# Two-block transformer kernel: the first modulation weights loaded into free rooms of the arena, and four chunks of the first projection multiplied between them

## The chip, the cores and the metric

The kernel runs on one core of a Trainium2 chip. The time is that of the device in microseconds, the median of a few executions. TensorE (PE in the profile) has two clock levels, 1.2 and 2.4 GHz.

## The reference

Two blocks follow one another on a sequence of 256 tokens of width 1024, all in float32. The first block has two layers. Each layer works on the 256 tokens `x` and on 256 context tokens `xc`, and each begins like this:

```python
shift, scale, gate = jnp.split(jax.nn.silu(c) @ p["w_ada"] + p["b_ada"], 3, axis=-1)
shift_c, scale_c, gate_c = jnp.split(jax.nn.silu(c_ctx) @ p["w_ada"] + p["b_ada"], 3, axis=-1)
h = _rmsnorm(x, p["norm_g"]) * (1.0 + scale[:, None, :]) + shift[:, None, :]
hc = _rmsnorm(xc, p["norm_g"]) * (1.0 + scale_c) + shift_c
hp = h @ p["w_in"]
```

`w_ada` is 1024 x 3072, `w_in` is 1024 x 2720. Then come a convolution branch, a Fourier branch, a gating branch and attention, an output projection and the gated residual. The second block has two layers of a gated feed-forward network, a mixer with sixteen heads, and another feed-forward network. The change touches only the first 50 us: from the first loads to the first two products with `w_in` of layer 0.

## The kernel before

**Tiles.** Features lie on the 128 partitions: `hT` holds the modulated input as 8 chunks (`KD` = 8) of 128 features by 512 tokens (256 of `x`, 256 of the context). A product of float32 precision is made of three products of split operands: each operand is a high part (rounded, `hH` for the input, `first_high` for weights) and a low part (`hL`, `first_low`, which lies in the place of the raw weights in the ring). `three` (L1893) issues high by high, high by low and low by high into one bank. ACT makes the high parts (`split_high`, L687, and L761, L763 for the input), DVE the low parts as the difference (`split_low`, L1196, and L1264). A plain float32 product of 128x512 is issued as one instruction and appears in the profile as two records.

**Loads.** All large weights go through `weight_ring`, three slots of 1 MB. SyncE (SP) fills them in the order of the list `SLOTS`; slot `n` waits until slot `n - 3` is used up (`fill`, L508). Layer 0 begins with eight slots of `w_ada` (the pairs `ADA_START` = 0, 4, 2, 6, two halves each), then come the slots of `w_in`, 256 columns each: first `a`, then `g`, `q`, `kv`/`kr` and so on. The small weights and constants are loaded by GpSimd (POOL), after it has seen `a` loaded (L586). `x` and the context are loaded by ScalarE's queue.

**Modulation.** For each pair of slots, PE multiplies silu(c) with it (`ada_half`, four products of 32 columns, L1877), ACT copies the result to SBUF (`ada_copy`, L685), PE transposes it (`ada_transposes`, L1890), DVE sums it (`ada_summed`, L1175). After two pairs one half of shift and scale is ready (`modulation`, L1192 and L1194): half 0, of pairs 0 and 4, serves the input chunks 0 to 3, half 1, of pairs 2 and 6, the chunks 4 to 7. Then ACT makes the even chunks of `hT` (L757, L758), DVE the odd ones (L1254, L1255), out of the transposes of the normalised rows, which PE makes (`x_transposes`, L1917) into the banks `XB`.

**PE's order** in layer 0 is written out by hand and each engine works strictly in its order:

```python
ada_products(*ADA_START[0]); ada_half(*ADA_START[1], 0); x_transposes([0, 1])
ada_half(*ADA_START[1], 1); ada_transposes(*ADA_START[0]); x_transposes([2, 3])
ada_transposes(*ADA_START[1]); ada_half(*ADA_START[2], 0); x_transposes([4])
ada_half(*ADA_START[2], 1); ada_half(*ADA_START[3], 0); ada_transposes(*ADA_START[2])
x_transposes([5]); ada_half(*ADA_START[3], 1); x_transposes([7])
ada_transposes(*ADA_START[3]); x_transposes([6]); warm(2)
```

(`;` stands for a line break here.) `warm(2)` is two plain products of the identity whose result nobody reads. After it `first_two` multiplies the two units of slot `a` (each 128 output features, 8 chunks of 3 products, 48 products in all), then the unit `g` follows, and so on.

Of the kernel before, what the change touches and what calls it, by code (L numbers as in the profile page):

```python
# [78 lines left out]
class Marks:  # L79


    def __init__(self, nc, ctx, table):
        self.nc, self.ctx, self.table = nc, ctx, table
        self.sems, self.counts = {}, {}
# [12 lines left out]
    def at(self, stage, *key):  # L97

        return self.sem(stage), self.table.get((stage,) + key, 1)
# [107 lines left out]
def program(nc, I, out, table):  # L207
    ctx = ExitStack()
    with ctx:
# [146 lines left out]

        def ada_slot(L, s):
            pair, q = s - s % 2, s % 2
            add(("ada", L, s), [(I["w_ada"][L][512 * q:512 * q + 512, 256 * pair:256 * pair + 512].rearrange("(k p) n -> p k n", p=P), ADA_WIDTH)])
# [8 lines left out]
        for L in range(2):  # L368
            win = [colslot(I["w_in"][L], c, n) for c, n in WIN_SLOTS]
            if L == 0:  # L370
                ada_slots(ADA_START)
# [48 lines left out]
        for L in range(2):  # L420
            for s in range(ADA_SLOTS):
                LAST[base[("ada", L, s)]] = ("ada_rows", L, s)
# [3 lines left out]
            for s in range(4):  # L426
                LAST[base[("wout", L)] + s] = ("wout_used", L, s, 1) if s < 3 else ("y_ready", "b1", L, 3 if L == 0 else 1, 1)
        def slot(n):
            return ring[:, n % RING, :]
# [77 lines left out]
        def _(sp):  # L507
# [61 lines left out]
            sp.wait_ge(M.sem("stored"), 64)  # L569
# [5 lines left out]
        def _(pool):  # L575
# [10 lines left out]
            pool.wait_ge(*filled(WIN[0, 0]))  # L586
# [84 lines left out]
        def _(act):  # L671
# [66 lines left out]
            def layer(L):  # L738
                nq = TT if L == 0 else T
                if L == 0:  # L740
                    norm(("b1", 0), range(4))
                    ada_copy(*ADA_START[0])
                    ada_copy(*ADA_START[1])
                else:
# [4 lines left out]
                for c in range(0, KD, 2) if L == 0 else ():  # L749
                    if c == 4:  # L750
                        ada_copy(*ADA_START[2])
                        ada_copy(*ADA_START[3])
                        split_high(0)
                        split_high(1)
# [4 lines left out]
                    if L == 0:  # L759
# [3 lines left out]
                        A(hH[:, c + 1, :], hT[:, c + 1, :], ACT.Copy).then_inc(*done("first_high", "input", c + 1))  # L763
                if L == 0:
# [393 lines left out]
        def _(dve):  # L1158
# [74 lines left out]
            def layer(L):  # L1233
# [616 lines left out]
        def _(pe):  # L1850
# [16 lines left out]
            def ada_half(L, s, q):  # L1867
# [6 lines left out]
                n = base[("ada", L, s + q)]  # L1874
                pe.wait_ge(*filled(n))
                for k in range(4):
                    last = mm(b[32 * k:32 * k + 32, :], CS[:, 4 * q + k, :], quarters(n)[:, k, :], start=(q == 0), stop=(q == 1), skip_group_check=True)  # L1877
# [29 lines left out]
            def layer(L):  # L1907
# [38 lines left out]

                if L == 0:
# [23 lines left out]
                hs = (hH, hL)  # L1971
# [11 lines left out]

                def first_two():
                    for j in range(2):
# [738 lines left out]
```

## Time and profile before

| | |
|---|---|
| median of 3 runs | 1441.98 us (1441.14 to 1442.56) |
| profiled execution: its own time | 1443.0 us |
| profiled execution: span of the core | 1441.2 us |
| PE busy | 1408.2 us, 98% of the span |
| VectorE (DVE) busy | 1004.8 us, 70% |
| ScalarE (ACT) busy | 717.2 us, 50% |
| GpSimd (POOL) busy | 72.1 us, 5% |
| granted clock of PE | 1.0 |

The span is the part of the execution that the profiler shows, 1.8 us shorter than the execution's own time. PE is busy nearly always. In the forty slices of the page only the first one (36 us) has it busy for half of the time.

### The profile page before, as it was taken

How to read it: one execution, taken by the hardware profiler on the slowest of the kernel's cores; microseconds unless marked ns; L12 is line 12 of the kernel's file. 1: busy time of each engine (PE TensorE's matmuls, PEld its weight loads, DVE VectorE, ACT ScalarE, POOL GpSimd, SP SyncE). 2: the span in 40 equal slices, each digit the busy share in tenths (PEclk: the TensorE clock that was granted, in tenths of full speed). 3: DMA queues.
4: the chain of work that ended last, by engine and by line, in shares of the span. 5: the costliest groups of instructions: out<-in, count | busy, mean ns of one | idle time of the engine just before them, and what ended most of it. 6: DMA issues, size and time to landing. Idle time of an engine off the chain costs nothing.

```text
span 1441.2 us, 22052 instructions
## 1 busy us (share of the span) xinstructions
PE 1408.2 (98%) x8031; PEld 1158.1 (80%) x8031; DVE 1004.8 (70%) x1669; ACT 717.2 (50%) x1228; POOL 72.1 (5%) x98
## 2 busy tenths in 40 slices
PE   5999999999999999999999999999999999999998
PEld 2768747869748888888878888888888888888887
DVE  2588455459547777787687777777777876877776
ACT  4433155345445444485764444654444756644444
POOL 0300211200110000000100000000000002000000
PEclk9999999999999999999999999999999999999999
DMA  9623175364235766554445556646665643455662
GB/s 344 210 88 88 59 254 192 99 198 143 88 118 165 245 194 202 196 184 125 146 132 175 175 178 201 203 145 198 201 199 175 191 140 124 132 175 176 202 201 91
DMA packets 185653, 243.28 MB, mean 169 GB/s; under 512 B 4560, under 2 KB 154608, under 8 KB 185456
## 3 DMA queue, kind: packets, MB, share of 16 engines
q1 hardware_dynamic: 182272, 229.43, 49.2%
q0 software_dynamic: 2736, 10.82, 2.2%
q10 hardware_dynamic: 576, 2.10, 0.4%
q8 instruction: 45, 0.74, 0.2%
q14 instruction: 24, 0.20, 0.0%
HBM read 241.27 MB, written 1.05 MB: 168 GB/s over the span
## 4 chain that ended last, share of the span: by engine, by line
PE 86%; DMA 4%; DVE 4%; ACT 3%; issue 2%; SPq 0%; POOL 0%; DVEq 0%; ACTq 0%; POOLq 0%
PE bank L1896 41%; PE bank L2412 18%; PE bank L2414 9%; DMA weight_ring<-in_w_ffn_up 2%; PE bank L2023 2%; PE bank L2304 2%; ACT weights_high L941 2%; DVE weights_low L1492 1%; DMA weight_ring<-in_w_ada 1%; PE bank L1877 1%; PE bank L2245 1%; PE bank L2168 1%; PE bank L2270 1%; PE bank L2254 1%; PE bank L2576 1%
## 5 line engine op out<-in xcount | busy, mean ns | idle before, releaser
L1492 DVE TENSOR_TENSOR weights_low<-weight_ring,weights_high 128x1024 fp32r<-128x1024 f32 x328 | 392.9, 1222 | 126.0 <-ACT weights_high L941 125.8
L941 ACT ACTIVATE weights_high<-weight_ring 128x1024 fp32r<-128x1024 f32 x328 | 334.6, 1048 | 100.4 <-PE bank L1896 62.0
L2412 PE MATMUL bank<-input_split,weights_high 128*128 128x512 f32 x1280 | 319.5, 391 | 0.0
L2412 PEld LDWEIGHTS bank<-input_split,weights_high 128*128 128x128 f32 x1280 | 234.7, 188 | 44.9
L2414 PEld LDWEIGHTS bank<-input_split,weights_low 128*128 128x128 f32 x1280 | 174.6, 190 | 12.5
L2414 PE MATMUL bank<-input_split,weights_low 128*128 128x256 f32 x1280 | 178.5, 282 | 0.0
L1896 PE MATMUL bank<-weights_high,hidden_high 128*128 128x512 f32 x352 | 138.7, 394 | 4.0 <-DVE hidden_low L1601 4.0
L1015 ACT ACTIVATE silu_gate<-gate_sum 128x256 f32<-128x256 f32 x88 | 36.8, 418 | 204.0 <-DVE gate_sum L1579 200.1
L1896 PE MATMUL bank<-weights_low,hidden_high 128*128 128x512 f32 x352 | 137.9, 392 | 0.0
L1896 PE MATMUL bank<-weights_high,hidden_low 128*128 128x512 f32 x352 | 137.0, 389 | 0.0
L1896 PE MATMUL bank<-input_split,weights_high 128*128 128x256 f32 x576 | 105.6, 285 | 0.0
L1021 ACT ACTIVATE hidden_high<-hidden 128x256 fp32r<-128x256 f32 x88 | 36.8, 418 | 131.4 <-DVE hidden L1592 124.4
L1896 PE MATMUL bank<-hT_high,first_high 128*128 128x512 f32 (+1 forms) x248 | 89.9, 362 | 1.3 <-DVE weight_ring_low L1198 1.1
L1896 PE MATMUL bank<-weights_high,input_split 128*128 128x256 f32 (+1 forms) x384 | 90.3, 323 | 0.5 <-issue 0.5
L1896 PEld LDWEIGHTS bank<-input_split,weights_high 128*128 128x128 f32 x576 | 89.5, 192 | 1.1 <-DVE qk_feature_major L1675 0.7
L1896 PE MATMUL bank<-hT_high,weight_ring_low 128*128 128x512 f32 (+1 forms) x248 | 86.9, 350 | 0.0
L1896 PE MATMUL bank<-input_split,weights_low 128*128 128x256 f32 x288 | 81.4, 283 | 0.0
L1896 PEld LDWEIGHTS bank<-weights_high,hidden_high 128*128 128x128 f32 x352 | 66.4, 189 | 17.1 <-issue 5.6
L1896 PEld LDWEIGHTS bank<-weights_high,hidden_low 128*128 128x128 f32 x352 | 66.1, 188 | 14.4
L1896 PEld LDWEIGHTS bank<-weights_low,hidden_high 128*128 128x128 f32 x352 | 66.4, 189 | 10.6
L1896 PEld LDWEIGHTS bank<-weights_high,input_split 128*128 128x128 f32 x384 | 64.4, 190 | 8.6 <-issue 3.5
L1601 DVE TENSOR_TENSOR hidden_low<-hidden,hidden_high 128x256 fp32r<-128x256 f32 x88 | 37.4, 425 | 43.7 <-ACT hidden_high L1021 43.7
(337 smaller groups left out, 2218.3 us busy)
## 6 DMA issues: line engine op xcount, KB each, us to landing
weight_ring<-in_w_ffn_gate SPq DMA_DIRECT2D x44, 1024.0 KB, 5.2
weight_ring<-in_w_ffn_up SPq DMA_DIRECT2D x44, 1024.0 KB, 5.3
weight_ring<-in_w_ffn_down SPq DMA_DIRECT2D x44, 1024.0 KB, 4.9
weight_ring<-in_w_in SPq DMA_DIRECT2D x32, 1024.0 KB, 5.3
weight_ring<-in_w_ada SPq DMA_DIRECT2D x24, 1024.0 KB, 5.7
weight_ring<-in_w_out SPq DMA_DIRECT2D x16, 1024.0 KB, 4.9
weight_ring<-in_w_in SPq DMA_DIRECT2D x24, 512.0 KB, 5.1
gain_row<-in_norm_gains POOLq DMA_DIRECT2D x6, 512.0 KB, 3.8
```

The costliest lines, as they stand in the source:

```text
L941: A(unit_in(WH, U), unit_source(U), ACT.Copy).then_inc(s_high, 1)
L1015: A(sgate[:, par, :], gsum[:, par, :], ACT.Silu).then_inc(s_silu, 1)
L1021: A(HBH[:, par if to is None else to, :], hbuf[:, par, :], ACT.Copy).then_inc(s_hh, 1)
L1492: TTn(unit_in(WL, U), unit_source(U), unit_in(WH, U).bitcast(F32), ALU.subtract).then_inc(s_low, 1)
L1601: TTn(HBL[:, to, :], hbuf[:, par, :], HBH[:, to, :].bitcast(F32), ALU.subtract).then_inc(s_hl, 1)
L1877: last = mm(b[32 * k:32 * k + 32, :], CS[:, 4 * q + k, :], quarters(n)[:, k, :], start=(q == 0), stop=(q == 1), skip_group_check=True)
L1896: last = mm(o, lhs(x), rhs(y), start=start and m == 0, stop=stop and m == 2, skip_group_check=True)
L2023: last = mm(b[out_rows, 0:ncol], lhs(k), hT[:, k, 0:ncol], start=(k == 0), stop=(k == KD - 1))
L2168: last = mm(b[:, sg * T:(sg + 1) * T], FA[:, 2 * sg + tl, m, cs * P:(cs + 1) * P], dft_n[:, cs, tl, :], start=(g == 0), stop=(g == 3))
L2304: last = mm(o, SG[:, k, tok], rows(n)[:, r, half], start=start, stop=final, skip_group_check=True)
L2412: mm(b[:, :].rearrange("p (h n) -> p h n", h=2), unit_in(WH, U)[:, k, :], HX[:, k, :, :], start=(k == 0), stop=False, skip_group_check=True)
L2414: last = mm(b[:, 0:T], unit_in(WL, U)[:, k, :], HH[:, k, :], start=False, stop=(k == KD - 1), skip_group_check=True)
```

## The change

The eight slots of `w_ada` for the start leave the ring. They go to five rooms of 2048 columns of `arena`, which hold nothing yet at this time: the first five need no wait, each of the last three waits until the slot five before it is multiplied. SP's order becomes: modulation slots 0 to 3, `a`, modulation slots 4 to 7, the constants `ones`, then `g` and `q` (no wait, as the ring is empty), then the others. POOL's loads now wait for the last modulation product and not for `a`. Five existing semaphores count the loads of the rooms; those who wait on them later add what the rooms have counted.

PE multiplies the first four input chunks with both units of `a` between the modulation products, in the order shown below. The transposes of chunk 7 move ahead of the last modulation half, `warm(2)` becomes five such products into bank 6, and after them the chunks 4 to 7 follow. ACT splits unit 0 of `a` before chunk 0 and unit 1 after the chunks 0 and 1, DVE makes the low parts in the same places, and `ada_summed` of the third pair moves to the fourth.

```diff
@@ loads
+        START = [(L, s + q) for L, s in ADA_START for q in range(2)]
+        START_ROOM = [arena[:, a:a + 2048] for a in (3840, 5888, 9592, 11640, 13688)]
+        START_SEMS = ("softplus_masked", "scores2", "p2_T", "pT2_ready", "stored")
...
+            def fill_start(i):
+                L, s = START[i]
+                if i >= 5:
+                    sp.wait_ge(*at("ada_rows", *START[i - 5]))
+                sp.dma_start(start_slot(i), ada_source(L, s)).then_inc(start_loaded[i % 5], 16)
+
+            for i in range(4):
+                fill_start(i)
             n_first = base[("ffn", 0)]
             for n in range(n_first):
                 fill(n, *SLOTS[n])
                 if n == WIN[0, 0]:
+                    for i in range(4, 8):
+                        fill_start(i)
                     sp.dma_start(KB[:, P:C_PICK], I["k_base"][:, P:C_PICK]).then_inc(M.sem("ones_loaded"), 16)
...
-            pool.wait_ge(*filled(WIN[0, 0]))
+            pool.wait_ge(*at("ada_rows", *START[-1]))
@@ ACT
                     ada_copy(*ADA_START[0])
                     ada_copy(*ADA_START[1])
+                    split_high(0)
...
                     if c == 4:
                         ada_copy(*ADA_START[2])
                         ada_copy(*ADA_START[3])
-                        split_high(0)
-                        split_high(1)
...
                         A(hH[:, c + 1, :], hT[:, c + 1, :], ACT.Copy).then_inc(*done("first_high", "input", c + 1))
+                        if c == 0:
+                            split_high(1)
@@ DVE
                     if L == 0 and c == 5:
+                        ada_summed(*ADA_START[2])
                         ada_summed(*ADA_START[3])
                         modulation(0, 1)
-                        split_low(0)
...
-                    if L == 0 and c == 3:
-                        ada_summed(*ADA_START[2])
-                    if L == 0 and c == 5:
-                        split_low(1)
+                    if L == 0 and c == 1:
+                        split_low(0)
...
+                    if L == 0 and c == 1:
+                        split_low(1)
@@ PE
+                def first_two(chunks, units=(0, 1)):
+                    w = [(first_high(j), first_low(j)) for j in range(2)]
+                    for j in units:
+                        if chunks[0] == 0:
+                            for r in hand_over(PB[0]["a", j], ("a_ready", 0, j)):
+                                pe.wait_ge(*at(*r))
+                            pe.wait_ge(*at("first_low", "weight", j))
+                        for k in chunks:
+                            pe.wait_ge(*at("first_low", "input", k))
+                            last = three(B[PB[0]["a", j]][:, :], lambda x: w[j][x][:, k, :], lambda y: hs[y][:, k, :], k == 0, k == KD - 1)
...
                     ada_transposes(*ADA_START[1])
+                    x_transposes([4])
                     ada_half(*ADA_START[2], 0)
-                    x_transposes([4])
+                    first_two((0, 1))
                     ada_half(*ADA_START[2], 1)
                     ada_half(*ADA_START[3], 0)
                     ada_transposes(*ADA_START[2])
                     x_transposes([5])
+                    x_transposes([7])
+                    first_two((2,))
                     ada_half(*ADA_START[3], 1)
-                    x_transposes([7])
+                    first_two((3,), (0,))
                     ada_transposes(*ADA_START[3])
+                    first_two((3,), (1,))
                     x_transposes([6])
-                    for r in hand_over(2):
+                    for r in hand_over(6):
                         pe.wait_ge(*at(*r))
-                    warm(2)
+                    for _ in range(5):
+                        mm(B[6][:, :], ident, X[:, 0, 0:512], start=True, stop=True)
+                    first_two((4, 5))
+                    first_two((6, 7))
```

## Rows read from the trace of the kernel before

**Rows 1.** The waits of PE over the whole span: us, times, longest us.

```profile
PE bank L1864 <- DMA const_base<-in_k_base: 9.7, 1, 9.7
PE bank L1877 <- DMA weight_ring<-in_w_ada: 4.3, 5, 1.8
PE bank L1896 <- DVE hidden_low L1601: 4.0, 3, 1.9
PE bank L1890 <- ACT ada_rows L685: 2.0, 2, 1.8
...
PE bank L1896 <- DVE weight_ring_low L1198: 1.1, 1, 1.1
```

**Rows 2.** The chain that ended last, in order of time: start, us.

```profile
4.51 13.13 DMA weight_ring<-in_w_ada
...
28.25 7.53 DMA weight_ring<-in_w_in
...
38.38 39.09 PE bank L1896 x168
```

**Rows 3.** Timeline of PE: start, us; idle before and its releaser in brackets.

```profile
21.55 1.94 PE L1877 MATMUL bank<-weight_ring,silu_c 128*32 128x512 f32 x8
...
26.54 0.66 PE L1917 MATMUL bank<-const_base,gated 128*128 128x128 f32 x4
27.13 1.07 PE L1877 MATMUL bank<-weight_ring,silu_c 128*32 128x512 f32 x8
28.78 1.07 PE L1877 MATMUL bank<-weight_ring,silu_c 128*32 128x512 f32 x8 [0.59 <-DMA weight_ring<-in_w_ada]
31.64 0.63 PE L1890 MATMUL bank<-const_base,ada_rows 128*128 128x128 f32 x4 [1.79 <-ACT ada_rows L685]
32.10 0.60 PE L1917 MATMUL bank<-const_base,gated 128*128 128x128 f32 x4
32.63 1.06 PE L1877 MATMUL bank<-weight_ring,silu_c 128*32 128x512 f32 x8
33.63 0.66 PE L1917 MATMUL bank<-const_base,gated 128*128 128x128 f32 x4
34.51 0.63 PE L1890 MATMUL bank<-const_base,ada_rows 128*128 128x128 f32 x4 [0.22 <-ACT ada_rows L685]
34.98 0.60 PE L1917 MATMUL bank<-const_base,gated 128*128 128x128 f32 x4
35.41 1.88 PE L1937 MATMUL bank<-residual,const_base 128*128 128x512 f32 x4
38.38 0.47 PE L1896 MATMUL bank<-hT_high,first_high 128*128 128x512 f32 x1 [1.08 <-DVE weight_ring_low L1198]
...
49.53 0.39 PE L1896 MATMUL bank<-hT_high,first_high 128*128 128x512 f32 x1
```

**Rows 4.** Stretches: us, busy PE, PEld, DVE, ACT, POOL, then granted clock, DMA share, GB/s.

```profile
20.00:24.00 4.00, 4.00 (x19) 2.00 (x18) 0.00 (x0) 0.45 (x1) 0.00 (x0) 1.00 1.05 388
24.00:28.00 4.00, 4.00 (x35) 2.11 (x33) 1.72 (x6) 1.68 (x4) 0.00 (x0) 1.00 1.03 342
28.00:32.00 4.00, 1.62 (x16) 0.58 (x13) 2.20 (x4) 3.28 (x7) 0.00 (x0) 1.00 0.98 307
```

**Rows 5.** Timelines of SP, then of ACT and DVE, 14 to 38 us.

```profile
14.36 0.37 SPq L518 DMA_DIRECT2D weight_ring<-in_w_ada  x1
...
23.55 0.60 ACT L685 ACTIVATE ada_rows<-bank 128x512 f32<-128x512 f32 x1 [4.87 <-PE bank L1877]
26.37 0.54 DVE L1254 TENSOR_SCALAR hT<-bank,ada_gain,ada 128x256 f32<-128x256 f32 x1
26.43 0.57 ACT L757 ACTIVATE hT<-bank,ada,ada_gain 128x256 f32<-128x256 f32 x1 [2.29 <-DVE ada_gain L1194]
27.48 0.63 ACT L761 ACTIVATE hT_high<-hT 128x512 fp32r<-128x512 f32 x1
28.14 1.29 DVE L1264 TENSOR_TENSOR hT_low<-hT,hT_high 128x512 fp32r<-128x512 f32 x2 [0.78 <-ACT hT_high L761]
35.68 0.17 DVE L1194 SCALAR_TENSOR_TENSOR ada_gain<-ada,vectors_T 128x8 f32<-128x8 f32 x1
35.81 2.00 ACT L691 ACTIVATE first_high<-weight_ring 128x1024 fp32r<-128x1024 f32 x2 [1.45 <-DMA weight_ring<-in_w_in]
36.90 1.23 DVE L1198 TENSOR_TENSOR weight_ring_low<-weight_ring,first_high 128x1024 fp32r<-128x1024 f32 x1 [1.05 <-ACT first_high L691]
```

**Rows 6.** Load issued at 14.36 us: KB, us from issue to landing.

```profile
weight_ring<-in_w_ada SPq DMA_DIRECT2D x1, 1024.0 KB, 6.0
```

More of the change, by code:

```diff
@@ L83, in __init__ @@
         self.nc, self.ctx, self.table = nc, ctx, table
-        self.sems, self.counts = {}, {}
+        self.sems, self.counts, self.start_count = {}, {}, {}
     def sem(self, stage):
@@ L355, in rows2, with ada_source @@
             return w.rearrange("(s r p) n -> s p r n", r=2, p=P)[s], 0
+        def ada_source(L, s):
+            pair, q = s - s % 2, s % 2
+            return I["w_ada"][L][512 * q:512 * q + 512, 256 * pair:256 * pair + 512].rearrange("(k p) n -> p k n", p=P)
         def ada_slot(L, s):
[L358 to L359 removed]
+            add(("ada", L, s), [(ada_source(L, s), ADA_WIDTH)])
         def ada_slots(pairs):
@@ L420, in program @@
         for L in range(2):
-            for s in range(ADA_SLOTS):
+            for s in range(8 if L == 0 else 0, ADA_SLOTS):
                 LAST[base[("ada", L, s)]] = ("ada_rows", L, s)
@@ L427, in program, with start_slot, start_filled @@
                 LAST[base[("wout", L)] + s] = ("wout_used", L, s, 1) if s < 3 else ("y_ready", "b1", L, 3 if L == 0 else 1, 1)
+        START = [(L, s + q) for L, s in ADA_START for q in range(2)]
+        START_ROOM = [arena[:, a:a + 2048] for a in (3840, 5888, 9592, 11640, 13688)]
+        START_SEMS = ("softplus_masked", "scores2", "p2_T", "pT2_ready", "stored")
+        start_loaded = [M.sem(stage) for stage in START_SEMS]
+        for i in range(len(START)):
+            M.start_count[START_SEMS[i % 5]] = 16 * (i // 5 + 1)
+        def start_slot(i):
+            return START_ROOM[i % 5].rearrange("p (k n) -> p k n", k=4)
+        def start_filled(i):
+            return start_loaded[i % 5], 16 * (i // 5 + 1)
         def slot(n):
@@ L1873, in ada_half @@
                 b = B[ADA_BANK[L, s]]
-                n = base[("ada", L, s + q)]
-                pe.wait_ge(*filled(n))
+                if (L, s) in ADA_START:
+                    i = START.index((L, s + q))
+                    pe.wait_ge(*start_filled(i))
+                    rows4 = start_slot(i)
+                else:
+                    pe.wait_ge(*filled(base[("ada", L, s + q)]))
+                    rows4 = quarters(base[("ada", L, s + q)])
                 for k in range(4):
-                    last = mm(b[32 * k:32 * k + 32, :], CS[:, 4 * q + k, :], quarters(n)[:, k, :], start=(q == 0), stop=(q == 1), skip_group_check=True)
+                    last = mm(b[32 * k:32 * k + 32, :], CS[:, 4 * q + k, :], rows4[:, k, :], start=(q == 0), stop=(q == 1), skip_group_check=True)
                 last.then_inc(*done("ada_rows", L, s + q))
@@ L1945, in spatial_transposes @@
                     last.then_inc(*done("ws_transposed", L))
+                hs = (hH, hL)
+                def first_two(chunks, units=(0, 1)):
[8 more added lines that the diff above has]
+                            last = three(B[PB[0]["a", j]][:, :], lambda x: w[j][x][:, k, :], lambda y: hs[y][:, k, :], k == 0, k == KD - 1)
+                        if chunks[-1] == KD - 1:
+                            last.then_inc(*done("proj", 0, "a", j))
                 if L == 0:
@@ L1982, in project_split @@
                     last.then_inc(*done("proj", 0, *key))
-                def first_two():
-                    for j in range(2):
-                        for r in hand_over(PB[0]["a", j], ("a_ready", 0, j)):
-                            pe.wait_ge(*at(*r))
-                    w = [(first_high(j), first_low(j)) for j in range(2)]
-                    for k, j in [(k, j) for ks in (range(0, 4), range(4, 6), range(6, 8)) for j in range(2) for k in ks]:
-                        if k == 0:
-                            pe.wait_ge(*at("first_low", "weight", j))
-                        if j == 0:
-                            pe.wait_ge(*at("first_low", "input", k))
-                        last = three(B[PB[0]["a", j]][:, :], lambda x: w[j][x][:, k, :], lambda y: hs[y][:, k, :], k == 0, k == KD - 1)
-                        if k == KD - 1:
-                            last.then_inc(*done("proj", 0, "a", j))
                 def project(name, j, n, lhs, out_rows, ncol, reader, first=False):
```

8 lines of the change are left out of this document (2 added, 6 removed).

## The prediction

> **What bounds the kernel now.** I read the waits of PE first [rows 1]. PE is busy 98% of the span, so only what shortens or lengthens PE's own order counts. Of its waits, 9.7 us are for the first constants and not touched. The change is aimed at some of the others, which lie in the first 40 us. The chain of waits [rows 2] shows why they are there. The chain runs through the loads, ends its last load with slot `a` landing at 28.25 + 7.53 = 35.78, passes through the split of unit 0, and from 38.38 on it is PE without a break for 39.09 us. Whatever moves PE's arrival at unit `g` (49.53, the last row of [rows 3]) moves the rest by the same amount. The later waits on the ring hang on PE's own releases, so they move along. I therefore build PE's new timeline up to unit `g` and compare it with 49.53.
>
> The stretches [rows 4] show that the loads run at 388 GB/s until 24 us and sag to 307 by 32: the ring of three makes SP wait for products. The timeline of PE [rows 3] shows what it does meanwhile. Its idle time after 25 us: 0.59 before the record at 28.78, 1.79 before 31.64, 0.22 before 34.51 and 1.1 before 38.38, some 3.7 us in all. That is the most the change can win here. Part of it is already used by two plain products: four records of 1.88 us together.
>
> **Where the loads land.** Row by row the third load lands at 4.51 + 13.13 = 17.64 [rows 2] and the fourth at 14.36 + 6.0 = 20.4 [rows 5, 6]: one megabyte per 2.72 us, which is 1.05 MB at 386 GB/s. The new order has no hole, so `a`, fifth in line, lands at 23.1, modulation slots 4 to 7 at 25.8, 28.5, 31.3 and 34.0, `ones` at 34.7, `g` at 37.5. The last modulation slot is thus later than in the old order (its product started at 32.63), since a megabyte was put ahead of it.
>
> **Up to the first early product.** Until 25.5 us nothing changes on PE. Then chunk 4's transposes (0.5) and modulation slot 4 (landed at 25.8, eight records, 1.07) end at about 27.1. The first early product needs the low parts of unit 0 and of chunk 0.
> ACT: the copy of the second pair ends at 23.55 + 0.60 = 24.15; the split of unit 0 takes 1.0 and ends at 25.25, before the gain is ready at 26.34, so it is hidden, with 1.1 us to spare if `a` should land later. hT of chunk 0 starts at 26.43, the high part at 27.48, that of chunk 1 ends at 28.63 [rows 5]. The split of unit 1 then ends at 29.7.
> DVE: chunk 1 from 26.37 to 27.36; low part of unit 0, 1.23, to 28.6; low parts of chunks 0 and 1, 0.65 each, to 29.25 and 29.9; low part of unit 1 needs ACT's at 29.7 and ends at 31.15.
> So PE starts unit 0 at 29.35, after 2.2 us idle, ends its two chunks at 30.75, waits 0.45 and starts unit 1 at 31.2. Behind that wait stand all later modulation products, although slot 5 lies ready since 28.5 us.
>
> **From 31.2 on PE has no hole.** Prices: 48 split products took 49.53 - 38.38 = 11.15 us, 0.232 each; a modulation half 1.04; transposes of a pair 0.45 and of a chunk 0.5 (starts of neighbouring rows); a plain product two records 0.43 apart, 0.86 [rows 3].
>
> - unit 1, chunks 0 and 1: 6 x 0.232 = 1.39, to 32.6
> - modulation slots 5 and 6: 2.08, to 34.7 (landed at 28.5 and 31.3; the copy of the third pair, from 33.7 to 34.35, is hidden by slot 6)
> - transposes of the third pair and of chunks 5 and 7: 1.45, to 36.15
> - chunk 2, both units: 1.39, to 37.55 (its low part is ready near 33 us, as ACT and DVE have nothing else)
> - modulation slot 7: 1.04, to 38.6. It landed at 34.0, so a delay of the loads up to 3.5 us costs nothing
> - chunk 3, unit 0: 0.70, to 39.3, which hides ACT's copy of 0.60
> - transposes of the last pair 0.45, chunk 3 of unit 1 0.70, transposes of chunk 6 0.45: to 40.9
> - five plain products: 5 x 0.86 = 4.3, to 45.2
> - chunks 4 to 7: 24 x 0.232 = 5.57, to 50.8
>
> That is 1.25 us later than 49.53.
>
> **Do the plain products fill a pause?** Chunk 4's low part is late by this chain: transposes of the last pair start at 39.3; in the old trace from there to the gain is 35.85 - 34.51 = 1.34 us; from the gain to chunk 4's low part is what it was for chunk 0: from 26.34 to 28.14 + 0.65 = 28.8, 2.45 us. ACT is free for it now, since the weight splits that took it from 35.81 to 37.81 are gone from this place. So chunk 4 is ready at 43.1. PE is free at 40.9. The pause is 2.2 us long and the products put into it last 4.3: they overfill it by 2.1 us. Without any of them PE would go on at 43.1 and reach `g` at 48.7, 0.8 us before the old time. Chunks 5 to 7 become ready in time: ACT and DVE need some 5.3 us from the gain to chunk 7, and PE asks for chunk 6 at 48.0.
>
> In terms of work: PE saves about 1.3 us of idle time, and gets three plain products more, 2.6 us.
>
> **Behind it.** The splits of unit `g` follow chunk 7 on ACT: near 45.3 to 47.4, low parts to 48.8, needed at 50.8: hidden. `g` and `q` land at about 37.5 and 40 to 42, before their splits. In the old order `q` landed near 49.6 and PE did not wait for it either, so the earlier landing wins nothing. POOL's small loads start after 38.6 and not at 36.08, 2.5 us later; nobody waited for them. SP's queue has no wait before slot `kv` that PE could feel. The rest keeps its order: shift +1.25 us.
>
> **The clock.** All stretches show a granted clock of 1.00 [rows 4], that is 2.4 GHz, but eight modulation records take 1.94 us at 21.55 and 1.07 at 27.13 [rows 3]; I go by the durations, which have the lower level before 24 us and the upper one after it. Between 27.13 and 31.64 the old order gave PE only sparse modulation products and 2.4 us of idle time, and the transposes at 31.64 still ran fast. The new hole from 27.1 to 29.35 is shorter than that stretch, so I take no fall. The Trainium skill ("TensorE: Matmul & The Clock Gate", the part on the clock gate) says that the throttled level is the default and that sustained activity releases it, which speaks for plain products in a pause and against a hole ahead of dense work; if it bit here the time would be that of the second rival below.
>
> **The rivals.**
>
> *First: the early chunks start earlier than I have them (gain).* If DVE and ACT fed PE from 27.1 on without a hole, the 12 products would end at 29.9, not 32.6, and slot 7 still lands in time (34.0 against 34.9), so `g` starts at 48.1: -1.4 us, 1440.6. For it: slot 4 is done at 27.1 and nothing else stands in PE's way. Against it: low parts cannot be there before 29.25 by the rows of ACT and DVE. Part of it, 0.5 us from a quicker unit 1, is thinkable.
>
> *Second: the clock falls in the hole at 27.1 (slower than before).* Place: the products from 29.35 on. Price: in the old trace the level rose after PE had been busy from 19.65 to 24, 4.3 us; that much work at half the rate adds 2.2 us, on top of 1.25: +3.4, 1445.4. It decides from 1.6 us of slow work's extra on. For it: 2.2 us idle after a sparse half. Against it: the old stretch named above, and the even longer sparse one after 28.
>
> *Third: the low parts come later than by my rows,* because ACT and DVE run into each other's waits or `a` lands late, after 24.2. Each microsecond beyond 1.1 of a late `a` shifts PE by one. At 2 us late, and a chunk 4 still covered by the plain products, 1444.2.
>
> *Fourth: something outside this window,* for example a ring or a queue that now runs half a step better or worse. No row speaks for it; both signs.
>
> **How the numbers follow.** The profiled execution took 1443.0, 1.0 above the median of 1441.98; its shift goes onto the median: 1441.98 + 1.25 = 1443.2 us. Chances: this case 0.62 (1442.4 to 1444.2); first rival, in whole or in part, 0.17 (1440.6 to 1442.4); second 0.08 (1444.6 to 1446.5); third 0.08 (1444 to 1446); fourth 0.05. A change of 0.2%, 2.9 us, is about what a measurement tells from none. My case lies within it. Slower by more than that needs the second rival or a strong third: 0.11. Faster by more is beyond the 1.4 us that PE's order can give and is left to the fourth and to an error in my timeline: 0.07. The range that holds 8 in 10 is 1440.9 to 1445.0.
>
> **What would show it right or wrong.** In the new profile: `a` landing near 23 and slot 7 near 34 us; the first early product at 29.3, unit 1's at 31.2; slot 7's product at 37.5, not at its landing; ten records of plain products from 40.9 to 45.2 with chunk 4's low part ready at 43.1, two us before they end; unit `g` at 50.8 without a wait. I am wrong if the low part of chunk 4 is later than the last plain product (then the pause was real and my chain from the last pair is too short), if eight modulation records take 1.9 us after 29, or if PE waits anew behind 50 us.

## The result, and the profile after

The changed kernel takes 1443.26 us (median of 22 runs, 1441.98 to 1446.42), the kernel before 1440.97 us (22 runs, 1439.47 to 1443.88). The ratio is 1.0016, with a 95% interval of 1.001 to 1.0022: 2.3 us slower (1.4 to 3.2 us by the interval). The forecast was 1443.2 us, a shift of 1.25 us. The time came out where it was forecast, but the shift is nearly twice as large and the forecast one lies just under the interval: the kernel before was 1.0 us faster over 22 runs than over the first three, and the forecast leaned on those three. One of the twelve executions of e1 below took 4949.69 us; it counts in e1's median and not in its ratio.

The timeline of PE in the profiled execution after (start, us; idle before in brackets), which answers to [rows 3]. L1907 is the modulation product, L1926 the split product, L1920 and L1947 the transposes, L2017 the five plain products:

```profile
21.55 1.44 PE L1907 MATMUL bank<-arena,silu_c 128*32 128x512 f32 x8
...
24.28 0.60 PE L1920 MATMUL bank<-const_base,ada_rows 128*128 128x128 f32 x4
...
26.23 1.07 PE L1907 MATMUL bank<-arena,silu_c 128*32 128x512 f32 x8 [0.91 <-DMA arena<-in_w_ada]
28.51 0.47 PE L1926 MATMUL bank<-hT_high,first_high 128*128 128x512 f32 x1 [1.22 <-DVE hT_low L1287]
...
31.74 1.92 PE L1907 MATMUL bank<-arena,silu_c 128*32 128x512 f32 x16
33.61 0.64 PE L1920 MATMUL bank<-const_base,ada_rows 128*128 128x128 f32 x4
34.09 1.04 PE L1947 MATMUL bank<-const_base,gated 128*128 128x128 f32 x8
...
36.45 1.06 PE L1907 MATMUL bank<-arena,silu_c 128*32 128x512 f32 x8
...
38.33 0.63 PE L1920 MATMUL bank<-const_base,ada_rows 128*128 128x128 f32 x4
...
39.50 0.60 PE L1947 MATMUL bank<-const_base,gated 128*128 128x128 f32 x4
39.93 4.46 PE L2017 MATMUL bank<-residual,const_base 128*128 128x512 f32 x10
43.83 0.79 PE L1926 MATMUL bank<-hT_high,first_high 128*128 128x512 f32 x1
...
49.78 0.39 PE L1926 MATMUL bank<-hT_high,first_high 128*128 128x512 f32 x1
```

PE waits 0.91 us for modulation slot 4, before 26.23, and 1.22 us before 28.51; from there on no wait is listed until unit `g` at 49.78 us. The forecast had one wait of 2.2 us behind slot 4; the slot came later than forecast (issued at 11.62 and 14.5 us on its way, so landed at 26.1, where 25.8 was forecast) and now splits it in two. The ten records of the five plain products run from 39.93 to past 44. The same execution's timeline of DVE shows when chunk 4 was ready:

```profile
41.48 1.29 DVE L1287 TENSOR_TENSOR hT_low<-hT,hT_high 128x512 fp32r<-128x512 f32 x2 [0.78 <-ACT hT_high L784]
```

Two low parts in 1.29 us: chunk 4's is there at 42.13, half of that later. PE was free for it at 39.93. The pause is 2.2 us long and is filled with 4.3 us.

The last modulation slot is issued at 20.54 us by the timeline of SP:

```profile
20.54 1.81 SPq L543 DMA_DIRECT2D arena<-in_w_ada  x1
```

and the view of the loads gives its time from issue to landing:

```profile
arena<-in_w_ada SPq DMA_DIRECT2D x1, 1024.0 KB, 13.7
```

It lands at 34.24 us and is multiplied at 36.45, because chunk 2's products stand in front of it.

Unit `g` starts only 0.25 us later than in [rows 3] (49.78 against 49.53). Part of that is luck of this execution. The eight modulation records at 21.55 took 1.44 us and not 1.94, and the transposes that start at 24.28 above stand at 25.02 in the timeline of PE before:

```profile
25.02 0.60 PE L1890 MATMUL bank<-const_base,ada_rows 128*128 128x128 f32 x4
```

So PE became fast earlier than in the profile of before, by about 1.5 us (an estimate: twice the 0.74 us by which it is ahead, as it works at half the rate until then). Single profiles are compared below only where the same row tells when the clock rose. Nor does the shift of 0.25 us simply run through to the end. In the chain of this pair it is 0.24 us at 96 us and 0.31 at 453; by 490 us, behind a stretch in which the chain runs through a load of `in_w_ffn_up`, it is -0.14, and at 1421 us -0.59.

A good marker of the end of the products with `a` is ACT's first read of their banks, 1.2 us ahead of unit `g`. In the timeline of ACT, before and after:

```profile
48.36 0.60 ACT L774 ACTIVATE arena<-bank 128x512 f32<-128x512 f32 x1 [3.53 <-PE bank L1896]
48.60 0.60 ACT L799 ACTIVATE arena<-bank 128x512 f32<-128x512 f32 x1 [2.35 <-PE bank L1926]
```

### The profile page after: what moved, and what is told of

Same layout as the page of the kernel before. It is cut to its first block, busy times and chain, and to the rows that moved or that the text cites. A ratio compares the mean times of both kernels' runs of the same rounds, so it can differ in the third digit from the quotient of the medians.

```text
span 1440.6 us, 22065 instructions
## 1 busy us (share of the span) xinstructions
PE 1409.9 (98%) x8037; PEld 1158.9 (80%) x8037; DVE 1005.4 (70%) x1669; ACT 717.3 (50%) x1228; POOL 72.1 (5%) x98
## 3 DMA queue, kind: packets, MB, share of 16 engines
HBM read 241.27 MB, written 1.05 MB: 168 GB/s over the span
## 4 chain that ended last, share of the span: by engine, by line
PE 86%; DVE 5%; ACT 3%; DMA 3%; issue 2%; SPq 0%; POOL 0%; DVEq 0%; ACTq 0%; POOLq 0%
PE bank L1926 41%; PE bank L2447 18%; PE bank L2449 9%; PE bank L2059 2%; DMA weight_ring<-in_w_ffn_up 2%; PE bank L2339 2%; DVE weights_low L1517 1%; ACT weights_high L966 1%; PE bank L1907 1%; PE bank L2280 1%; DMA arena<-in_w_ada 1%; PE bank L2203 1%; PE bank L2305 1%; PE bank L2289 1%; PE bank L2611 1%
## 5 line engine op out<-in xcount | busy, mean ns | idle before, releaser
L1926 PE MATMUL bank<-weights_high,hidden_high 128*128 128x512 f32 x352 | 138.7, 394 | 3.1 <-DVE hidden_low L1626 3.1
L1926 PE MATMUL bank<-weights_low,hidden_high 128*128 128x512 f32 x352 | 137.9, 392 | 0.0
L1926 PE MATMUL bank<-weights_high,hidden_low 128*128 128x512 f32 x352 | 137.0, 389 | 0.0
L1926 PE MATMUL bank<-input_split,weights_high 128*128 128x256 f32 x576 | 105.6, 285 | 0.0
L1926 PE MATMUL bank<-hT_high,first_high 128*128 128x512 f32 (+1 forms) x248 | 90.7, 366 | 1.4 <-DVE hT_low L1287 1.2
L1926 PE MATMUL bank<-weights_high,input_split 128*128 128x256 f32 (+1 forms) x384 | 90.2, 323 | 0.5 <-issue 0.5
L1926 PEld LDWEIGHTS bank<-input_split,weights_high 128*128 128x128 f32 x576 | 89.6, 192 | 1.1 <-DVE qk_feature_major L1700 0.7
L1926 PE MATMUL bank<-hT_high,weight_ring_low 128*128 128x512 f32 (+1 forms) x248 | 86.9, 350 | 0.0
L1926 PE MATMUL bank<-input_split,weights_low 128*128 128x256 f32 x288 | 81.4, 283 | 0.0
L1926 PEld LDWEIGHTS bank<-weights_high,hidden_high 128*128 128x128 f32 x352 | 66.4, 189 | 16.2 <-issue 4.6
L1926 PEld LDWEIGHTS bank<-weights_high,hidden_low 128*128 128x128 f32 x352 | 66.1, 188 | 14.4
L1926 PEld LDWEIGHTS bank<-weights_low,hidden_high 128*128 128x128 f32 x352 | 66.4, 189 | 10.6
L1926 PEld LDWEIGHTS bank<-weights_high,input_split 128*128 128x128 f32 x384 | 64.4, 190 | 8.6 <-issue 3.5
```

Source lines behind the costliest of these rows:

```text
L1926: last = mm(o, lhs(x), rhs(y), start=start and m == 0, stop=stop and m == 2, skip_group_check=True)
```

## The experiments

Eleven runs, nine altered kernels and both kernels once more, stand in three groups (e1 to e4, e5 to e8, e9 to e11), each group on one chip and in five rounds beside the kernel before. The marker is ACT's first read of unit `a`'s bank; "eight records" is the length of the modulation product at 21.6 us, 1.94 where the clock rose late. Each execution also has a mean granted clock, rounded to 0.001; an estimate of its worth is at most 1.4 us for each 0.001, as 0.001 of 1441 us of PE's time. At most, since it also holds the last 2 to 3 us, where PE runs out of work and the clock falls too (0.97 from 1420 to 1440 us in the first profile after, 1.00 in the one before).

| | median us | ratio (95% interval) | marker us | eight records us |
|---|---|---|---|---|
| before (first profile) | | | 48.36 | 1.94 |
| after (first profile) | 1443.26 | 1.0016 (1.001 to 1.0022) | 48.60 | 1.44 |
| e1 no plain product | 1442.59 | 1.0005 (0.9995 to 1.0014) | 49.02 | 1.94 |
| e2 two plain | 1441.25 | 1.0000 (0.999 to 1.001) | 47.35 | 1.94 |
| e3 before, five plain | 1443.98 | 1.0017 (1.0008 to 1.0027) | 49.07 | 1.63 |
| e4 slot 7 first | 1440.15 | 0.9994 (0.9986 to 1.0003) | 46.00 | 1.91 |
| e5 after, again | 1443.71 | 1.0015 (1.0006 to 1.0024) | 49.72 | 1.21 |
| e6 before, again | 1441.76 | 1.0003 (0.9994 to 1.0012) | 47.91 | 1.62 |
| e7 slots 5 and 7 first | 1440.59 | 0.9987 (0.9978 to 0.9996) | 47.23 | 1.26 |
| e8 products late | 1442.83 | 1.0006 (0.9997 to 1.0015) | 49.80 | 1.94 |
| e9 one in the hole | 1442.64 | 1.0002 (0.9992 to 1.0011) | 48.61 | 1.36 |
| e10 slot 7 first, held | 1440.17 | 0.9983 (0.9974 to 0.9991) | 45.52 | 1.56 |
| e11 late, held | 1442.19 | 0.9993 (0.9985 to 1.0002) | 47.31 | 1.33 |

The kernel before has a median of its own in each group (1441.69, 1441.90 and 1442.15), so the ratios are to be compared, not the medians.

### e1 and e2: how many plain products the pause wants

```diff
-                    for _ in range(5):
+                    for _ in range(0):   # e1; range(2) in e2
```

> The changed kernel without any of the five plain products in the pause. Theory A (the pause is 2.2 us and the five products of 0.86 us overfill it): in the profile of after PE reaches the pause at 39.93 us and chunk 4's low part is ready at 42.13, while the products end near 44.2; without them the next split product starts at 42.1 to 42.3 and everything behind moves by 2.1 us: about 1441.2 us, ratio to before 0.9995 to 1.0005. Rival B (the products keep the clock up): PE falls to the lower level in the empty 2.2 us, the 24 split products behind it take more than 0.25 us each at first, and the time is no better than with five, 1443 us or more. Rival C (the slowdown comes from elsewhere, later than 50 us): the unit g starts 2.1 us earlier in the profile, but the time stays at 1.0016 of before.

> The changed kernel with two plain products in the pause, as many as before the change. Theory A: two products last 1.72 us, from 39.93 to 41.65, less than the pause, so the time is that of the kernel without any, 2.1 us under the changed one: about 1441.2 us. If Rival B holds, two are better than none by the cost of the fallen clock, 1 us or more.

With two, the ratio is 1.0000: 1.6 thousandths under the changed kernel, 2.3 us, where 2.1 was expected. PE waits 0.41 us behind the two products, and the marker stands at 47.35, with the late rise, 1.0 us ahead of before; no gain over the kernel before shows in the time. With none, the pause is as long (a wait of 2.23 us, below), but the times fall into two heaps, seven from 1440.3 to 1442.9 and four from 1444.7 to 1445.3. The profile is of the upper heap (1445.13 us). Its stretches (us, busy PE, PEld, DVE, ACT, POOL, then granted clock, DMA share, GB/s) show the clock falling behind the pause:

```profile
43.00:44.00 1.00, 0.98 (x4) 0.85 (x5) 1.00 (x3) 0.97 (x3) 1.00 (x3) 1.00 0.97 391
44.00:45.00 1.00, 1.00 (x4) 0.77 (x3) 0.98 (x2) 0.83 (x3) 1.00 (x2) 0.58 0.94 287
45.00:46.00 1.00, 1.00 (x3) 0.74 (x3) 0.69 (x1) 1.00 (x3) 1.00 (x3) 0.50 0.72 129
46.00:47.00 1.00, 1.00 (x4) 0.77 (x3) 0.96 (x1) 0.94 (x2) 1.00 (x3) 0.50 1.09 223
47.00:48.00 1.00, 1.00 (x5) 0.83 (x4) 1.00 (x2) 0.00 (x0) 1.00 (x2) 0.71 0.81 195
```

and the timeline of PE in it shows the price:

```profile
43.02 0.47 PE L1926 MATMUL bank<-hT_high,first_high 128*128 128x512 f32 x1 [2.23 <-DVE hT_low L1287]
...
45.18 0.63 PE L1926 MATMUL bank<-hT_low,first_high 128*128 128x512 f32 x1
45.60 0.63 PE L1926 MATMUL bank<-hT_high,weight_ring_low 128*128 128x512 f32 x1
46.03 0.63 PE L1926 MATMUL bank<-hT_high,first_high 128*128 128x512 f32 x1
```

Split products are 0.43 us apart instead of 0.23, for some 3.3 us: the clock fell to 1.2 GHz after the empty pause. Marker 49.02 against 47.35 in e2, 1.7 us for it. The pause doesn't explain the heaps, though. The same profile has a second fall, behind a wait of PE in the later block:

```profile
506.88 0.49 PE L1926 MATMUL bank<-weights_high,hidden_high 128*128 128x512 f32 x1 [2.00 <-DVE hidden_low L1626]
```

```profile
508.00:510.00 2.00, 2.00 (x7) 1.57 (x6) 2.00 (x3) 0.19 (x1) 0.00 (x0) 0.59 0.94 313
510.00:512.00 2.00, 2.00 (x6) 1.53 (x5) 1.68 (x4) 0.55 (x2) 0.00 (x0) 0.55 0.93 304
```

And ten of the eleven executions have a mean clock of 0.998 or less, against 11 of the 35 of the kernel before, so the first fall probably belongs to most of them, those of the lower heap too. So Theory A holds for the length of the pause, and Rival B for the clock in it: plain products in the pause are worth having, two do it, three more are paid in full.

### e3: the plain products alone

```diff
-                    warm(2)
+                    warm(5)
```

> The kernel before with five plain products in place of two, nothing else of the change. Theory A: in the old trace two products end at 37.1 us and the first split product starts at 38.38; five would end at 35.41 + 4.3 = 39.7, so +1.3 us: 1442.3 us, ratio 1.0009. If plain products are worth something for the clock in this pause, the time is that of before or under it.

1.0017; the interval from 1.0008 holds the expected 1.0009 just. In the profile the marker is 49.07 against 47.91 in e6, whose clock rose at the same time: +1.16 us. Three more of them cost what they last, less the rest of the pause, in the old kernel too. The time moved by about twice that, 2.4 us by the ratio, with a granted clock of 1.00 in its profile from the rise to 1440 us. So a time that moves by more than the marker isn't peculiar to the changed kernel.

### e4: the order of PE

```diff
-                    first_two((2,))
                     ada_half(*ADA_START[3], 1)
-                    first_two((3,), (0,))
+                    first_two((2,), (0,))
                     ada_transposes(*ADA_START[3])
-                    first_two((3,), (1,))
+                    first_two((2,), (1,))
+                    first_two((3,))
...
-                    for _ in range(5):
+                    for _ in range(0):
```

> The changed kernel with no plain product and with the last modulation half ahead of chunk 2's products; the products of chunks 2 and 3 then stand behind it and cover the chain from its transposes to chunk 4. Theory A': PE is the bound from 28.5 us on and what was badly used was the order. Slot 7 landed at 34.2 us, its product starts at 34.9 and not at 36.45, its pair's transposes near 36.6, chunk 4's low part is ready near 40.4, PE is free at 39.4 to 39.7. So about 0.9 us of pause remain and unit g starts near 46.3 us, 3.3 us before the kernel before: about 1437.7 us, ratio 0.9977, 1.4 us or so under the version without plain products. Rival B: the clock falls in the holes and the time is above 1440. Rival C: the start of unit g moves but the time does not.

The timeline of PE in e4 shows the last modulation product earlier:

```profile
35.71 1.06 PE L1907 MATMUL bank<-arena,silu_c 128*32 128x512 f32 x8
...
37.58 0.63 PE L1920 MATMUL bank<-const_base,ada_rows 128*128 128x128 f32 x4
```

With the late rise the marker is 46.00, 2.4 us before the old one and 1.35 before e2 (expected 1.4). In the time the ratio is 0.9994: the expected 0.9977 lies outside the interval. The gain at the marker is real, but the time doesn't show it clear of noise; four of the twelve executions took 1441.9 to 1443.2.

### e5 and e6: both kernels once more

> The changed kernel once more, unaltered, beside the controls of this call. Theory D (the forecast's shift of 1.0 to 1.3 us is right and the measured 2.3 us is scatter of the later stages): ratio near 1.0009. Theory E (the clock also falls or rises late in some executions of it, as it did at 44 us without plain products): ratio again 1.0014 to 1.0020, with two heaps of times 2 us apart.

> The kernel before, unaltered: a control of how far two equal kernels come out apart. Expected ratio 1.0000, within 0.0005. Its profile is a second look at the old timeline: if the clock rises earlier than 24 us there, unit a ends earlier by as much of it as the loads do not absorb.

The control gives 1.0003. Its clock rose earlier than in the first profile of the same kernel, PE is 0.54 us ahead at 25 us, and the marker is 0.45 us earlier: the loads absorb little of it. The changed kernel gives 1.0015 again (the interval, from 1.0006, also holds the forecast 1.0009), so a slowdown of this order isn't scatter of one group. Its second profile shows what the first did not, in the same view of stretches:

```profile
27.00:28.00 1.00, 0.33 (x4) 0.00 (x0) 1.00 (x2) 1.00 (x3) 0.00 (x0) 1.00 1.06 389
28.00:29.00 1.00, 0.66 (x3) 0.54 (x4) 1.00 (x3) 1.00 (x2) 0.00 (x0) 0.89 1.06 391
29.00:30.00 1.00, 1.00 (x4) 0.81 (x3) 1.00 (x2) 0.97 (x3) 0.00 (x0) 0.50 1.05 385
30.00:31.00 1.00, 1.00 (x4) 0.80 (x3) 1.00 (x3) 0.36 (x2) 0.00 (x0) 0.50 1.05 387
31.00:32.00 1.00, 1.00 (x4) 0.72 (x3) 0.90 (x2) 0.51 (x1) 0.00 (x0) 0.50 1.05 389
```

and the timeline of PE in that profile:

```profile
28.34 0.47 PE L1926 MATMUL bank<-hT_high,first_high 128*128 128x512 f32 x1 [1.01 <-DVE hT_low L1287]
...
29.38 0.63 PE L1926 MATMUL bank<-hT_high,first_high 128*128 128x512 f32 x1
29.81 0.63 PE L1926 MATMUL bank<-hT_low,first_high 128*128 128x512 f32 x1
```

This is the second rival of the prediction, in the place named there. Before it PE had done the sparse product of slot 4 and waited 1.12 us before and 1.01 us behind it. From the first split product to the modulation product behind the twelve it takes 4.51 us (28.34 to 32.85) and not 3.23 (28.51 to 31.74), so the fall costs 1.3 us. The marker is 49.72, 1.1 us behind the first profile of the same kernel, although the clock had risen earlier. Theory E's fall is there, but its two heaps are not: ten of the eleven times lie between 1442.5 and 1444.5 us, none more than 0.6 us from the next.

How often does it happen? Up to there the order of PE is the same in five profiles (the two of the changed kernel, e1, e2 and e4), and this is the only one of them with a fall at this place. In e1, e2 and e4, where the clock rose late, the wait was even longer, 1.69 to 1.76 us, and every stretch of 4 us from 20 to 40 us has 1.00. In e2:

```profile
29.15 0.47 PE L1926 MATMUL bank<-hT_high,first_high 128*128 128x512 f32 x1 [1.73 <-DVE hT_low L1287]
```

The mean clocks of all executions tell the same: 0.99873 on average over the eleven of e5 and 0.99915 over the 33 beside them of the kernel before. The difference is worth 0.6 us by the estimate above, no more.

### e7: slot 5 ahead of the early products too

```diff
+                    ada_half(*ADA_START[2], 1)
                     first_two((0, 1))
-                    ada_half(*ADA_START[2], 1)
...
-                    for _ in range(0):
+                    for _ in range(1):
```

(against e4.)

> As e4 (last modulation half ahead of chunk 2), and modulation slot 5 ahead of the first early products, with one plain product. Slot 5 lands at 28.8 us, its product ends at 29.9 when the first split product could have begun at 29.2; unit 1's low part, ready at 30.8, no longer makes a hole. Slot 7's product starts 0.5 us earlier than in e4, and so does everything behind: unit a ends 0.5 us earlier than in e4, time 1439.6 us. If the hole at 27.4 to 28.8 lets the clock fall, split products from 30 us on take 0.43 us each and it is slower than e4.

The expected order came about, but in the profiled execution the clock fell in the hole, now 1.5 us long and between two sparse products. The timeline of PE:

```profile
26.42 1.06 PE L1907 MATMUL bank<-arena,silu_c 128*32 128x512 f32 x8 [1.10 <-DMA arena<-in_w_ada]
29.03 1.94 PE L1907 MATMUL bank<-arena,silu_c 128*32 128x512 f32 x8 [1.54 <-DMA arena<-in_w_ada]
```

The second takes 1.94 us where the first takes 1.06, and the marker is 47.23 instead of 45.5. The ratio, 0.9987, is about the expected one all the same: its times reach from 1437.7 to 1442.3, wider than those of e10 below.

### e8 and e11: the loads alone, and with the clock held

e8 takes out every early product and puts `first_two((0, 1, 2, 3))` behind the last transposes, without plain products. e11 adds two plain products behind the modulation products of slots 4 and 5 each:

```diff
                     ada_half(*ADA_START[2], 0)
+                    for r in hand_over(6):
+                        pe.wait_ge(*at(*r))
+                    for _ in range(2):
+                        mm(B[6][:, :], ident, X[:, 0, 0:512], start=True, stop=True)
                     ada_half(*ADA_START[2], 1)
+                    for r in hand_over(6):
+                        pe.wait_ge(*at(*r))
+                    for _ in range(2):
+                        mm(B[6][:, :], ident, X[:, 0, 0:512], start=True, stop=True)
                     ada_half(*ADA_START[3], 0)
```

> The loads, rooms and the ACT and DVE order of the change, but no early product: all 48 split products of unit a stand together behind the last transposes, without plain products. Theory A': the last modulation half starts at its landing, 34.3 us, the 24 products of chunks 0 to 3 (5.6 us) cover the chain of 4.5 us to chunk 4, unit g starts near 48.1 us, 1.4 us before the old place and 1.5 to 2 us before the changed kernel: about 1440.0 us. Then the loads' order alone is worth 1.4 us and the early products of the change as placed cost. Rival (the early products are what can win): 1442 us or more.

> e8 (all split products of unit a at the end) with two plain products behind modulation slot 4's product and two behind slot 5's. In e8's profile the clock fell at 31.5 us for about 6 us and the bank of unit a was read at 49.8 us, not at the expected 46.7. Theory A' with the clock held: about 47.0 us for that read, time 1440.3 us or less, ratio 0.9990. If the loads' order is worth nothing even so, 1441.7 or more.

e8 missed: 1.0006, and in its profile the stretches from 32 to 40 have the lower clock:

```profile
28.00:32.00 4.00, 1.20 (x12) 0.32 (x16) 4.00 (x7) 3.33 (x7) 0.00 (x0) 0.87 1.05 386
32.00:36.00 4.00, 4.00 (x19) 2.34 (x18) 1.42 (x3) 1.08 (x2) 0.00 (x0) 0.50 1.07 369
36.00:40.00 4.00, 3.18 (x20) 1.41 (x19) 0.25 (x2) 0.60 (x1) 1.49 (x3) 0.78 1.12 348
```

All its eleven executions have a mean clock of 0.999 or less. In e11 every stretch from 20 to 52 us has 1.00, and the marker is 47.31, 2.5 us before e8 and 0.6 before e6, whose clock rose a little later. The ratio, 0.9993, is near the expected 0.9990, but its interval also holds no change, and the median, 1442.19 us, is that of the kernel before beside it (1442.15) and on the side of "worth nothing". So the order of the loads by itself is worth little: some 0.5 us at the marker and 1 us by the ratio, not clear of noise. What e8 lost, the early products of the other versions save: they keep PE busy between the sparse modulation products.

### e9 and e10: the hole filled

e9 is the changed kernel with one plain product between slot 4's product and the first early product. e10 is e4 with two there, and one in the pause before chunk 4.

```diff
                     ada_half(*ADA_START[2], 0)
+                    for r in hand_over(6):
+                        pe.wait_ge(*at(*r))
+                    for _ in range(1):   # e9; range(2) in e10
+                        mm(B[6][:, :], ident, X[:, 0, 0:512], start=True, stop=True)
                     first_two((0, 1))
```

> The changed kernel with one plain product more, in the hole between modulation slot 4's product (ends 27.3 us) and the first early product (28.3 to 29.2), which is longer than its 0.86 us. Theory E (the changed kernel loses about 1 us on average because the clock falls in this hole in some executions, as in the second profile of it, split products 0.43 us apart from 28.9 to 32.1): the product is hidden and keeps the clock, so the profile has a granted clock of 1.00 from 24 to 56 us and the time falls by about 1 us, to 1442.4 us, ratio 1.0008. If the hole has nothing to do with it, the time stays at 1443.3 to 1443.7.

> The order of e4 (last modulation half ahead of chunk 2's products), two plain products in the first hole and one in the pause before chunk 4, none of the five. Theory E: unit a ends where it did in e4 (its bank read at 46.0 us, 2.4 before the old place), or 0.1 to 0.3 us later where two products overfill the hole, and in no execution does the clock fall there: about 1439.2 us, ratio 0.9983, and fewer times above 1442 than in e4.

e9 has more work than the changed kernel and gives 1.0002 (expected 1.0008) against 1.0016 and 1.0015; its interval ends at 1.0011. By the medians it is 1.1 us under e5, which ran on the same chip, the microsecond that was expected. Part of the distance in the ratios comes from the other side: the kernel before beside e9 had a lower mean clock than beside e5, 0.99883 and 0.99915. The marker is at 48.61, where the changed kernel has it when its clock holds, so the added product costs nothing. The granted clock is 1.00 in all stretches from 20 to 52 us. The timeline of PE shows the product, two records, and no wait behind it:

```profile
26.31 1.07 PE L1907 MATMUL bank<-arena,silu_c 128*32 128x512 f32 x8 [0.98 <-DMA arena<-in_w_ada]
27.30 1.13 PE L2005 MATMUL bank<-residual,const_base 128*128 128x512 f32 x2
```

e10 is the fastest by its ratio, 0.9983 (0.9974 to 0.9991), as expected: 2.4 us under the kernel before (2.0 by the medians). It and e7 are the versions whose intervals lie under 1. None of its twelve executions exceeds 1442.1. Its clock is 1.00 up to 56 us; its profile has its fall only later, behind a wait of 1.95 us at 469.67 us, like the second one of e1. In the timeline of ACT the marker:

```profile
45.52 0.60 ACT L799 ACTIVATE arena<-bank 128x512 f32<-128x512 f32 x1 [0.44 <-PE bank L1926]
```

## Why the prediction was right, and where not

**The time.** 1443.26 us against 1443.2 is luck: the baseline of three runs was 1.0 us too high and the shift 1.05 us too small, and the two errors cancel. What was right is the sign and, at the marker, the size.

**What bounds the kernel.** Right up to 450 us and only roughly behind it. PE has no new wait behind 50 us, but its waits there do not keep their length: those for `hidden_low` sum to 4.0 us in the profile before and 3.1 after. So a shift at unit `g` does not move the rest by exactly the same amount, as the prediction had it, and the markers order the kernels only loosely by time (e8 has the last marker, 49.80, and a ratio of 1.0006).

**The loads.** Right: `a` landed at 6.58 + 16.8 = 23.4 us (forecast 23.1), the last slot at 34.24 (34.0), in both cases before their users. Slot 7 lay ready for 2.2 us before its product; the forecast slack was 3.5 us (the product was forecast for 37.5).

**The first early product** came at 28.51, 0.84 before the forecast, mostly since the clock had risen earlier; in the profiles with the late rise it came at 29.15 to 29.17, 0.2 before the forecast. Unit 1's hole of 0.45 us shrank to 0.23: its products start at 30.20, 0.46 us behind the last start of unit 0, where the distance is otherwise 0.23. DVE's low part of unit 1 ended at 30.10, because records of ACT and DVE that follow one another overlap by 0.1 us each, which the sum by durations missed.

**The sum from there to unit `g`** was forecast as 21.45 us (29.35 to 50.8) and measured as 21.27 (28.51 to 49.78); with the hole of 0.23 us in place of 0.45 it would have been 21.23.

**The plain products.** Right, and the main point. The pause was forecast as 2.2 us and was 2.2. Taking out three of the five gives 2.3 us back (2.1 forecast), 1.9 to 2.0 of them at the marker (47.35 in e2 against 48.60 + 0.7).

**The clock.** Here a step failed. "I take no fall" was argued from the stretch of 27.13 to 31.64 in [rows 3], which is sparser and longer. The changed kernel does fall in some executions, at the place of the second rival; e5 shows one such execution, in which seven distances of 0.43 us in place of 0.23 cost 7 x 0.2 = 1.4 us (1.3 measured to the next modulation product). The price of the rival, 2.2 us, was too high: it was counted from 19.65 us, where the trace shows PE without a wait from 17.78 on. The version with that hole filled, e9, is faster by 1.3 thousandths in the ratio and 1.1 us in the median, though the intervals overlap. The mechanism was given a chance of 0.08 as an all or nothing case, where it happens in one execution and not in the next. What the rows of one profile say of the clock is one throw. The rule that the throttled level is the default and activity releases it (the Trainium skill, "TensorE: Matmul & The Clock Gate", the part on the clock gate), pointed the right way and this case's traces agree: 0.50 after the empty pause in e1, 1.00 with two products in it in e2.

**The rivals.** The first, a gain from early chunks, did not come about in this order of PE. The third, late low parts, did not either. The first guess of what PE's order can give at most, 1.4 us, was too small: it left the modulation halves behind chunk 2's products. With slot 7 first it is 2.4 us at the marker (e4), not all of it seen in the time.

**What stays open.** Of the 2.3 us, about 0.9 is the sum of the prediction as it shows at the marker (brought to the same rise: 48.60 + 0.7 against 48.36). The clock in the hole adds 0.3 us on average if one execution in five loses 1.3 us there, and 0.6 at most by the mean clocks of e5 and the executions beside it. The four executions of the changed kernel whose mean clock reads 1.000 took 1442.4 to 1442.6 us; the thirteen such of the kernel before beside e5 have a median of 1441.25, which is 1.3 us less, about the forecast shift. So the clock explains only a part of the excess, and some 1 us has no shown cause. It may be noise, since the interval reaches down to 1.4 us, or something behind 50 us, as e3 also moved the time by twice its shift at the marker. How many of the changed kernel's executions lose the clock isn't known, since a profile shows one.

Executions of one kernel differ by some 4 us. The clock is part of it: it falls in later stages as well, at 508 us in e1 and at 470 in e10, each time behind a wait of 2 us for `hidden_low`; beside e5, the kernel before has a median of 1441.25 at a mean clock of 1.000 and 1443.31 at 0.998. It is not all of it: from the products at 606 us to those at 1421 us, the same work in all kernels, the profiles of before and of e3 take 815.0 and 816.1 us without any fall.

## What to carry to other kernels

Where one engine works through an order written by hand, early work belongs into the holes of that order, behind what is already there and feeds a long chain, and not ahead of it; here the last modulation half should have come before the early products of chunk 2. Filler in a pause is to be measured against the length of the pause: in this one of 2.2 us, two products held the clock and five cost 2 us. And a pause is judged over many executions, since one profile may show the clock held where the next one shows it fallen.

## What the runs showed of the hardware

A hole as short as 1.01 us between sparse modulation products and dense work was followed by a granted clock of 0.50 for some 3 us in one execution (e5) and by 1.00 in others (1.22 us in the first profile, 1.69 to 1.76 in e1, e2 and e4). So the length of the hole alone did not decide it. The granted clock is not the whole story either: before 22 to 24 us it reads 1.00 while products take twice their later time, and the point at which they become fast lay about 1.5 us apart in profiles of the two kernels.

SP was held by its own issues. The first four megabytes were issued within 3.12 us; the fifth megabyte's issue took 5.00 us and the sixth's 5.28, where the first took 0.47, by the timeline of SP in the first profile after:

```profile
6.58 5.00 SPq L532 DMA_DIRECT2D weight_ring<-in_w_in  x1
11.62 5.28 SPq L543 DMA_DIRECT2D arena<-in_w_ada  x1
```

Nothing was lost by it here, because SP had nothing else to issue and the loads went on at 386 and 387 GB/s in the stretches from 24 to 32 us. What the free rooms gave was the sag of [rows 4] filled: the ninth megabyte lands at 34.24 us, against 35.78 in [rows 2].
